# Moving part of a modulation product from TensorE to VectorE in a two-block transformer kernel

## The chip, the cores and the metric

One Trainium2 chip, one core. The metric is the device time in microseconds of one execution. The profile below is of one profiled execution of the kernel before.

## The reference, cut to what matters

Two transformer blocks run one after the other over 256 tokens of 1024 features, each of depth 2. The first block scales, shifts and gates its norms and branches with six vectors per layer that come from a single row `c` (1 x 1024) times a wide matrix:

```
for l in range(2):
    mod = c @ mod_w[l] + mod_b[l]                     # 1024 x 6144 per layer
    sh1, sc1, g1, sh2, sc2, g2 = split(mod, 6)
    h = rmsnorm(x, norm1_g[l]) * (1 + sc1) + sh1
    x = x + g1 * mixer(h, ...)
    h = rmsnorm(x, norm2_g[l]) * (1 + sc2) + sh2
    x = x + g2 * conv_ffn(h, w_up[l], ..., w_down[l])
```

All of it is float32, and the large products are made as three products of rounded halves (high x high, low x high, high x low).

## The kernel before, in words

`plan()` writes a list of steps; each engine walks the same list and executes its part of each step, so the order of the list is the order on every engine. Weights come from HBM in chunks of 1 MB, one DMA each, into a ring of 5 buffers (`RING`); SyncE issues the load of chunk c when chunk c-5 has been read. A chunk holds two weight blocks of 8 sub-matrices of 128 x 128. ScalarE rounds a block to `w_hi` (L1649) and VectorE subtracts to make `w_lo` (L2042); 6 blocks are held (`SPLIT`), and a block's place comes free only when the whole output tile that read it last is done. So in the down projection a burst of two or three splits follows the end of each tile.

A modulation chunk (the step `mod`) is another kind of 1 MB chunk: 1024 rows x 256 columns of `mod_w`, for one layer l, one of the six vectors g and a part 0 to 3 of it. TensorE multiplies `c` with it straight from the ring in 8 float32 matmuls of 32 columns, four side by side in the array (L1435); ScalarE copies the bank to `modacc` (L1698). After part 3, ScalarE writes the four rows to HBM with a 16 KB DMA (L1703, tile `mod_rows`). A later step, `modload`, is a DMA on ScalarE's queue that first waits until that write has landed and then reads the rows back transposed (L1710, tile `modv`); the step `modsum` on VectorE adds the four quarters and the bias.

These chunks are dealt out as filler by `some_mod`: one after each tile `dn` j of layer 0's down projection (j = 0 to 7, 22 sub-matrices each, 66 matmuls), two around each norm by `gap_mod`, one at places in the attention. `reduce_mod` puts `modload` or `modsum` into the list where the next `some_mod` or stage boundary is. Between the tiles stand the `stat` steps: ScalarE squares a finished tile of x (L1683), GpSimd adds the squares. After dn 7 comes `root` (TensorE sums over partitions, ScalarE L1688 and L1690, VectorE L2150 to L2156) and `norm` of layer 1 (VectorE L2182, ScalarE L1746), after which TensorE starts the products of layer 1. VectorE's x update of a finished dn tile is L2413.

At the very start of the kernel two modulation chunks are already multiplied by VectorE: 8 instructions over the row blocks of a chunk, one after another because each adds to the last (L2119, L2121, L2122).

## Time and profile before

| what | value |
|---|---|
| time, median of 3 runs (lowest to highest) | 1541.74 us (1539.85 to 1541.89) |
| the profiled execution: its own time | 1542.8 us |
| the profiled execution: span, mean granted TensorE clock | 1541.0 us, 0.993 |
| TensorE busy | 1496.3 us, 97% of the span |
| VectorE busy | 1143.7 us, 74% |
| ScalarE busy | 833.4 us, 54% |
| GpSimd busy | 31.4 us, 2% |
| layer 0's down projection, first to last x update of a tile | 403.13 to 465.43 us |

Busy shares say which engine carries the most work over the whole run; an idle stretch of TensorE is time lost only where it stands between two pieces of its own work. The windows and the timeline show this stage by stage.

### The profile page before, as it was taken

How to read it: one execution, taken by the hardware profiler on the slowest of the kernel's cores; microseconds unless marked ns; L12 is line 12 of the kernel's file. 1: busy time of each engine (PE TensorE's matmuls, PEld its weight loads, DVE VectorE, ACT ScalarE, POOL GpSimd, SP SyncE). 2: the span in 40 equal slices, each digit the busy share in tenths (PEclk: the TensorE clock that was granted, in tenths of full speed). 3: DMA queues.
4: the chain of work that ended last, by engine and by line, in shares of the span. 5: the costliest groups of instructions: out<-in, count | busy, mean ns of one | idle time of the engine just before them, and what ended most of it. 6: DMA issues, size and time to landing. Idle time of an engine off the chain costs nothing.

```text
span 1541.0 us, 31309 instructions
## 1 busy us (share of the span) xinstructions
PE 1496.3 (97%) x12608; PEld 1433.5 (93%) x12608; DVE 1143.7 (74%) x2202; ACT 833.4 (54%) x1509; POOL 31.4 (2%) x36
## 2 busy tenths in 40 slices
PE   6999999999999999999999999999999999999997
PEld 4898898999998999989999989999999999999997
DVE  5758566888646586769996678878966988888774
ACT  3655545655435646446555655645555754645453
POOL 0000001000000000010001000000000000000000
PEclk9999999999999999999999999999999999999998
DMA  9654555676776452454545543443446444444430
GB/s 393 251 216 184 202 223 192 219 275 247 275 272 252 168 214 87 157 196 165 179 179 194 219 164 113 169 185 138 154 152 246 150 154 163 167 163 141 169 129 28
DMA packets 47840, 290.51 MB, mean 189 GB/s; under 512 B 9992, under 2 KB 12296, under 8 KB 13136
## 3 DMA queue, kind: packets, MB, share of 16 engines
q1 hardware_dynamic: 38880, 280.83, 49.0%
q10 hardware_dynamic: 8816, 7.67, 1.5%
q8 instruction: 101, 1.65, 0.4%
q14 instruction: 43, 0.35, 0.1%
HBM read 286.09 MB, written 2.39 MB: 187 GB/s over the span
## 4 chain that ended last, share of the span: by engine, by line
PE 57%; DVE 1%; ACT 1%; DMA 0%; issue 0%; DVEq 0%; ACTq 0%
PE bank L1351 17%; PE bank L1357 16%; PE bank L1352 16%; PE bank L1601 2%; PE sums L1526 1%; PE sums L1416 1%; PE bank L1390 1%; PE bank L1395 1%; PE bank L1389 1%; PE bank L1508 1%; PE bank L1499 1%; DMA mem_x<-mem_t 0%; DVE w_lo L2042 0%; ACT w_hi L1649 0%; PE bank L1533 0%
## 5 line engine op out<-in xcount | busy, mean ns | idle before, releaser
L1351 PE MATMUL bank<-h_hi,w_hi 128*128 128x256 f32 x2256 | 632.8, 288 | 8.9 <-ACT h_hi L1746 3.7
L1352 PE MATMUL bank<-h_hi,w_lo 128*128 128x256 f32 x2256 | 622.3, 283 | 0.0
L2042 DVE TENSOR_TENSOR w_lo<-ring,w_hi 128x1024 fp32r<-128x1024 f32 x436 | 523.4, 1222 | 106.4 <-ACT w_hi L1649 103.8
L1357 PE MATMUL bank<-h_lo,w_hi 128*128 128x256 f32 x2256 | 575.9, 283 | 0.0
L1649 ACT ACTIVATE w_hi<-ring 128x1024 fp32r<-128x1024 f32 x436 | 449.2, 1054 | 131.4 <-PE bank L1357 130.9
L1351 PEld LDWEIGHTS bank<-h_hi,w_hi 128*128 128x128 f32 x2256 | 432.8, 192 | 22.9 <-issue 17.9
L1352 PEld LDWEIGHTS bank<-h_hi,w_lo 128*128 128x128 f32 x2256 | 433.0, 192 | 0.6 <-issue 0.5
L1357 PEld LDWEIGHTS bank<-h_lo,w_hi 128*128 128x128 f32 x2256 | 405.2, 192 | 0.0
L1351 PE MATMUL bank<-a_hi,w_hi 128*128 128x256 f32 x352 | 99.6, 283 | 1.0 <-DVE w_lo L2042 0.7
L1352 PE MATMUL bank<-a_hi,w_lo 128*128 128x256 f32 x352 | 98.3, 279 | 0.0
L1357 PE MATMUL bank<-a_lo,w_hi 128*128 128x256 f32 x352 | 98.2, 279 | 0.0
L1389 PE MATMUL bank<-w_hi,h_hi 128*128 128x256 f32 (+1 forms) x304 | 86.6, 289 | 3.9 <-ACT h_hi L1746 2.9
L1390 PE MATMUL bank<-w_lo,h_hi 128*128 128x256 f32 (+1 forms) x304 | 85.7, 286 | 0.0
L1883 ACT ACTIVATE conv_a<-bank,sm 128x256 f32<-128x256 f32 x44 | 24.8, 564 | 105.2 <-PE bank L1357 105.2
L1395 PE MATMUL bank<-w_hi,h_lo 128*128 128x256 f32 (+1 forms) x304 | 81.7, 287 | 0.0
L1351 PE MATMUL bank<-y_hi,w_hi 128*128 128x256 f32 x288 | 79.3, 280 | 0.0
L1352 PE MATMUL bank<-y_hi,w_lo 128*128 128x256 f32 x288 | 78.8, 278 | 0.0
L1357 PE MATMUL bank<-y_lo,w_hi 128*128 128x256 f32 x288 | 75.7, 281 | 0.0
L1944 ACT ACTIVATE sig<-bank 128x256 f32<-128x256 f32 x80 | 30.3, 379 | 78.1 <-PE bank L1357 77.5
L1351 PEld LDWEIGHTS bank<-a_hi,w_hi 128*128 128x128 f32 x352 | 66.1, 188 | 4.7 <-issue 3.3
L1389 PEld LDWEIGHTS bank<-w_hi,h_hi 128*128 128x128 f32 x304 | 59.6, 196 | 7.2 <-issue 5.9
L1352 PEld LDWEIGHTS bank<-a_hi,w_lo 128*128 128x128 f32 x352 | 66.2, 188 | 0.0
(336 smaller groups left out, 2345.7 us busy)
## 6 DMA issues: line engine op xcount, KB each, us to landing
ring<-weights SPq DMA_DIRECT2D x266, 1024.0 KB, 4.9
pos_bias<-scratch ACTq DMA_DIRECT2D x4, 512.0 KB, 5.6
x<-x_t ACTq DMA_DIRECT2D x1, 1024.0 KB, 6.9
scratch<-line ACTq DMA_DIRECT2D x1, 1024.0 KB, 5.6
mem_x<-mem_t ACTq DMA_DIRECT2D x1, 1024.0 KB, 6.7
mem_second<-mem_t ACTq DMA_DIRECT2D x1, 1024.0 KB, 6.2
out_t<-x SPq DMA_DIRECT2D x2, 512.0 KB, 2.6
co<-const SPq DMA_DIRECT2D x1, 462.0 KB, 7.2
```

The source lines that it names most:

```text
L1351: pe.matmul(to, WH[:, b % SPLIT, o, :], hi[:, k, :], start=(i == 0), stop=False)
L1352: pe.matmul(to, WL[:, b % SPLIT, o, :], hi[:, k, :], start=False, stop=False)
L1357: last = pe.matmul(to, WH[:, b % SPLIT, o, :], lo[:, k, :], start=False, stop=(i == n - 1))
L1389: pe.matmul(o, q, WH[:, s:s + m.n, k, :], start=(k == 0), stop=False)
L1390: pe.matmul(o, q, WL[:, s:s + m.n, k, :], start=False, stop=False)
L1395: last = pe.matmul(o, q, WH[:, s:s + m.n, k, :], start=False, stop=(k == KD - 1))
L1416: m = pe.matmul(sums[:, 0:S], ones, hb[:, k, :], start=(st.n is None and k == 0), stop=(k == KD - 1))
L1601: m = pe.matmul(to[:, (2 * g + s) * P:(2 * g + s + 1) * P], k[half, g, s * P:s * P + P], q[half, g, t * P:t * P + P], start=True, stop=True)
L1649: act.activation(WH[:, b % SPLIT], ring_half(b), ACT.Copy).then_inc(w_hi, 1)
L1883: act.activation(to[:, st.j % 3, :], bank[u.bank][:, 0:S], ACT.Identity, scale=ss(("conv_w", st.l, 2), c), bias=ss(("conv_b", st.l), c)).t ...
L1944: act.activation(sig2[:, st.j % 4, :], bank[st.ps.bank][:, 0:S], ACT.Tanh, scale=0.5).then_inc(taken[st.ps.bank], 1)
L2042: ve.tensor_tensor(WL[:, b % SPLIT], ring_half(b), WH[:, b % SPLIT].bitcast(F32), ALU.subtract).then_inc(w_lo_v, 1)
```

## The change

`mod` has a second form, `by_vector`, in which VectorE multiplies and adds the 8 row blocks of the chunk and leaves 128 partial sums per column in `modacc`. A new step `modrow`, put into the list at the next `some_mod`, adds these over the partitions with one float32 matmul against ones, and ScalarE copies the bank back to `modacc` with a factor 0.25, since `modsum` adds four rows. `gap_mod` does nothing while such a chunk is open, and `some_mod` returns early when its `mod_row` has completed a vector. It is asked for in layer 0's down projection for j < 6.

```
+BY_VECTOR = 6
...
-    def mod(l, g, part):
+    def mod(l, g, part, by_vector=False):
...
+        n = p.count("mod_rows") if part == 3 else p.counts.get("mod_rows", 0)
+        more = dict(v=p.count("mod_v"), eng="vector") if by_vector else dict(ps=p.full_bank(), after=state["parts"])
+        st = p.add("mod", chunk=len(p.chunks) - 1, l=l, g=g, part=part, n=n, **more)
+        if by_vector:
+            state["row"] = st
+            return
...
+    def mod_row():
+
+        st, state["row"] = state["row"], None
+        if st:
+            row = p.add("modrow", l=st.l, g=st.g, part=st.part, n=st.n, v=st.v, ps=p.full_bank(), after=state["parts"])
+            state["parts"].append(row.ps)
+            if st.part == 3:
+                state["summed"] = (st.l, st.g)
...
-    def some_mod(n=1):
+    def some_mod(n=1, by_vector=False):
         reduce_mod()
+        mod_row()
+        if state["summed"]:
+            return
         for _ in range(min(n, len(queue))):
             l, g, part = queue.pop(0)
-            mod(l, g, part)
+            mod(l, g, part, by_vector)
...
     def gap_mod():
-        if queue and not state["summed"]:
+        if queue and not state["summed"] and not state["row"]:
             mod(*queue.pop(0))
...
             ps = fm("dn", dn[j], j=j, l=l).ps
-            some_mod()
+            some_mod(by_vector=l == 0 and j < BY_VECTOR)
...
+            def modrow(st):
+                to = claim(st.ps)
+                pe.wait_ge(mod_v, st.v + 1)
+                pe.matmul(to[:, 0:256], ones, modacc[:, st.part, :], start=True, stop=True).then_inc(ready, 1)
...
+            def modrow(st):
+                wait_ready(act, st.ps)
+                act.activation(modacc[:, st.part, :], bank[st.ps.bank][:, 0:256], ACT.Copy, scale=0.25).then_inc(
+                    taken[st.ps.bank], 1)
+                if st.part == 3:
+                    for u in st.after:
+                        wait_taken(act, u)
+                    act.dma_start(mod_rows.ap()[st.n], modacc[0:97:32, :, :]).then_inc(mod_row_out, 16)
...
             def mod(st):
                 if st.eng != "vector":
                     return
+                if st.n is not None:
+                    ve.wait_ge(mod_row_out, 16 * st.n)
                 wait_loaded(ve, st.chunk)
```

ScalarE from the evacuation after dn 6 to the norm of layer 1, before (L1698 is the copy of a modulation bank, L1683 a square, L1688 the root's logarithm, L1710 the read-back):

```order
L1698 ACTIVATE modacc<-bank 128x256 [waits bank_ready]
L1703 DMA mod_rows<-modacc 4x1024 [waits bank_taken1,bank_taken3,bank_taken6,bank_taken4]
L1683 ACTIVATE h_val<-x 128x256 [waits bank_taken0]
L1649 ACTIVATE w_hi<-ring 128x1024 [waits bank_ready,chunk_loaded1]
L1649 ACTIVATE w_hi<-ring 128x1024 [waits bank_ready,chunk_loaded2] x2
L1710 DMA modv<-mod_rows 128x4x8 [waits mod_summed,mod_row_out]
L1698 ACTIVATE modacc<-bank 128x256 [waits mod_row_out,bank_ready]
L1683 ACTIVATE h_val<-x 128x256 [waits bank_taken2]
L1683 ACTIVATE h_val<-x 128x256 [waits bank_taken4]
L1688 ACTIVATE guess<-sums,co 128x256 [waits sums_ready]
```

The same stretch now (L1716 is the copy of a `modrow` bank, L1729 that of a modulation bank, L1734 the write of the rows, L1741 the read-back, L1705 a square, L1710 the logarithm):

```order
L1716 ACTIVATE modacc<-bank 128x256 [waits bank_ready]
L1729 ACTIVATE modacc<-bank 128x256 [waits bank_ready]
L1705 ACTIVATE h_val<-x 128x256 [waits bank_taken5]
L1671 ACTIVATE w_hi<-ring 128x1024 [waits bank_ready,chunk_loaded4]
L1671 ACTIVATE w_hi<-ring 128x1024 [waits bank_ready,chunk_loaded2] x2
L1729 ACTIVATE modacc<-bank 128x256 [waits bank_ready]
L1734 DMA mod_rows<-modacc 4x1024 [waits bank_taken2,bank_taken4,bank_taken1,bank_taken6]
L1705 ACTIVATE h_val<-x 128x256 [waits bank_taken0]
L1705 ACTIVATE h_val<-x 128x256 [waits bank_taken3]
L1741 DMA modv<-mod_rows 128x4x8 [waits mod_summed,mod_row_out]
L1710 ACTIVATE guess<-sums,co 128x256 [waits sums_ready]
```

The write of the rows of vector 4 has moved from after dn 6 to after dn 7, and its read-back from before the last two squares to directly before the logarithm.

VectorE at dn 5 and dn 6, before (L2413 is the x update of a tile; L2047 on `modv` is `modsum`, which stood between the x updates of dn 4 and dn 5):

```order
L2413 SCALAR_TENSOR_TENSOR x<-bank,modv,x 128x256 [waits bank_ready,mod_summed]
L2042 TENSOR_TENSOR w_lo<-ring,w_hi 128x1024 [waits w_hi_done] x3
L2413 SCALAR_TENSOR_TENSOR x<-bank,modv,x 128x256 [waits bank_ready]
L2042 TENSOR_TENSOR w_lo<-ring,w_hi 128x1024 [waits w_hi_done] x3
L2413 SCALAR_TENSOR_TENSOR x<-bank,modv,x 128x256 [waits bank_ready]
L2042 TENSOR_TENSOR w_lo<-ring,w_hi 128x1024 [waits w_hi_done] x4
L2047 TENSOR_TENSOR modv<-modv 128x16 [waits mod_cols_in]
```

Now (L2446 is the x update, L2073 the low halves, L2152 to L2155 the new product, L2078 on `modv` is `modsum`):

```order
L2446 SCALAR_TENSOR_TENSOR x<-bank,modv,x 128x256 [waits bank_ready]
L2073 TENSOR_TENSOR w_lo<-ring,w_hi 128x1024 [waits w_hi_done] x3
L2078 TENSOR_TENSOR modv<-modv 128x16 [waits mod_cols_in]
L2078 TENSOR_TENSOR modv<-modv 128x8 [waits vector_order]
L2078 TENSOR_TENSOR modv<-modv,sm 128x8 [waits vector_order]
L2152 TENSOR_SCALAR modacc<-ring,sm 128x256 [waits chunk_loaded2,mod_row_out,mod_summed]
L2154 SCALAR_TENSOR_TENSOR modacc<-ring,sm,modacc 128x256 [waits vector_order] x6
L2155 SCALAR_TENSOR_TENSOR modacc<-ring,sm,modacc 128x256 [waits vector_order]
L2446 SCALAR_TENSOR_TENSOR x<-bank,modv,x 128x256 [waits bank_ready]
L2073 TENSOR_TENSOR w_lo<-ring,w_hi 128x1024 [waits w_hi_done] x3
L2446 SCALAR_TENSOR_TENSOR x<-bank,modv,x 128x256 [waits bank_ready]
L2073 TENSOR_TENSOR w_lo<-ring,w_hi 128x1024 [waits w_hi_done] x4
```

The product stands behind the splits of its tile, and after dn 5 behind `modsum` of vector 2 as well. There are five such products, after dn 0, 1, 2, 4 and 5: after dn 3 the step `modrow` completes vector 2 and no chunk is taken. `modsum` of vector 4, which stood right before the root's VectorE part, now comes after the first rotation of layer 1's queries.

TensorE after dn 6, now (L1446 is the sum over the partitions, L1457 the modulation matmul, L1368 and L1374 those of the down projection):

```order
L1374 MATMUL bank<-a_lo,w_hi 128x256
L1446 MATMUL bank<-modacc,co 128x256 [waits mod_by_vector,bank_taken1]
L1457 MATMUL bank<-ring,c_wide 32x256 [waits chunk_loaded0,c_wide_ready,bank_taken2]
L1457 MATMUL bank<-ring,c_wide 32x256 x7
L1368 MATMUL bank<-a_hi,w_hi 128x256 [waits w_lo_by_vector,bank_taken3]
```

Before, one group of 8 modulation matmuls stood after each of dn 0 to 7; now there is an L1446 after dn 1, 2, 3, 5 and 6, and a group of 8 after dn 6 and dn 7. All modulation chunks that follow move down the list by one to three steps, and the last of them, which stood in the gap of layer 1's second norm, now stands after the second tile of the up projection.

## Rows read from the trace of the kernel before

**Rows 1.** The page: busy time, share of the span and instructions of each engine.
```profile
PE 1496.3 (97%) x12608; PEld 1433.5 (93%) x12608; DVE 1143.7 (74%) x2202; ACT 833.4 (54%) x1509; POOL 31.4 (2%) x36
```
**Rows 2.** VectorE's timeline, down projections of layers 0 and 1: start us, us, what.
```profile
456.53 0.48 DVE L2413 SCALAR_TENSOR_TENSOR x<-bank,modv,x 128x256 f32<-128x256 f32 x1 [4.95 <-PE bank L1357]
456.93 3.49 DVE L2042 TENSOR_TENSOR w_lo<-ring,w_hi 128x1024 fp32r<-128x1024 f32 x3
465.43 0.48 DVE L2413 SCALAR_TENSOR_TENSOR x<-bank,modv,x 128x256 f32<-128x256 f32 x1 [5.01 <-PE bank L1357]
...
858.66 0.48 DVE L2413 SCALAR_TENSOR_TENSOR x<-bank,modv,x 128x256 f32<-128x256 f32 x1 [4.95 <-PE bank L1357]
...
866.37 0.48 DVE L2413 SCALAR_TENSOR_TENSOR x<-bank,modv,x 128x256 f32<-128x256 f32 x1 [3.82 <-PE bank L1357]
```
**Rows 3.** TensorE's timeline at a float32 sum over the partitions (two matmuls, second block).
```profile
1027.69 0.70 PE L1582 MATMUL bank<-conf_out,co 128*128 128x256 f32 x2
1028.23 0.59 PE L1583 MATMUL bank<-conf_out,co 128*128 128x256 f32 x2
...
1028.78 0.28 PE L1352 MATMUL bank<-h_hi,w_lo 128*128 128x256 f32 x1
```
**Rows 4.** VectorE's timeline at the start: a modulation chunk multiplied by VectorE.
```profile
13.40 0.35 DVE L2119 TENSOR_SCALAR modacc<-ring,sm 128x256 f32<-128x256 f32 x1 [4.42 <-DMA ring<-weights]
13.79 3.09 DVE L2121 SCALAR_TENSOR_TENSOR modacc<-ring,sm,modacc 128x256 f32<-128x256 f32 x6
...
17.31 0.15 DVE L2047 TENSOR_TENSOR modv<-bank,sm 128x2 f32<-128x2 f32 x1
```
**Rows 5.** VectorE's timeline at both `modsum`, and GpSimd's at the first.
```profile
441.40 0.81 DVE L2047 TENSOR_TENSOR modv<-modv 128x16 f32<-128x16 f32 x2
...
470.37 0.37 DVE L2047 TENSOR_TENSOR modv<-modv 128x16 f32<-128x16 f32 x2
...
441.45 0.74 POOL L1246 TENSOR_TENSOR mean<-mean,h_val 128x256 f32<-128x256 f32 x1 [7.13 <-ACT h_val L1683]
```
**Rows 6.** Three 1 MB loads issued within 1 us: their time to landing.
```profile
L1309 SPq DMA_DIRECT2D ring<-weights x3: 328/423/424, 450.5 to 451.4; - x3
...
DMA to landing us min/median/max: 4.8/6.9/8.9
```
**Rows 7.** ScalarE's timeline from dn 6 to the norm of layer 1.
```profile
459.45 0.36 ACT L1698 ACTIVATE modacc<-bank 128x256 f32<-128x256 f32 x1
459.92 0.50 ACTq L1703 DMA_DIRECT2D mod_rows<-modacc  x1
460.46 0.42 ACT L1683 ACTIVATE h_val<-x 128x256 f32<-128x256 f32 x1 [0.65 <-ACT modacc L1698]
...
468.61 0.71 ACT L1683 ACTIVATE h_val<-x 128x256 f32<-128x256 f32 x2
470.23 0.47 ACT L1688 ACTIVATE guess<-sums,co 128x256 f32<-128x256 f32 x1 [0.91 <-PE sums L1416]
```
**Rows 8.** The line of the read-backs: all ten, and their time to landing.
```profile
L1710 ACTq DMA_DIRECT2D modv<-mod_rows x10: 361/362/381, 135.1 to 693.7; - x10
...
DMA to landing us min/median/max: 1.8/3.9/5.4
```
**Rows 9.** VectorE's timeline: the root's first instruction at that norm.
```profile
471.05 0.42 DVE L2150 TENSOR_SCALAR mean<-sums 128x256 f32<-128x256 f32 x1
```
**Rows 10.** TensorE's timeline: its restart after that norm, and a wait in layer 1's up projection.
```profile
474.05 0.36 PE L1389 MATMUL bank<-w_hi,h_hi 128*128 128x256 f32 x1 [2.00 <-ACT h_hi L1746]
...
699.53 0.38 PE L1351 MATMUL bank<-h_hi,w_hi 128*128 128x256 f32 x1 [1.35 <-DVE w_lo L2042]
```
**Rows 11.** Windows: busy us (instructions) of PE, PEld, DVE, ACT, POOL, then PEclk, DMA share, GB/s.
```profile
471.00:475.20 4.20, 2.20 (x29) 1.57 (x22) 3.88 (x11) 1.79 (x5) 0.00 (x0) 0.99 1.00 419
475.20:478.40 3.20, 3.20 (x17) 3.20 (x16) 3.20 (x10) 2.07 (x5) 0.00 (x0) 0.50 1.04 440
```

More of the change, by code:

```diff
@@ L188, in plain @@
         return p.matrix([tile_cols(name, lead, [(c0 + P * j, P)], rows) for j in range(n)])
-    state = dict(parts=[], summed=None, loaded=None, added={}, all_by_pe={})
-    def mod(l, g, part):
+    state = dict(parts=[], summed=None, loaded=None, added={}, all_by_pe={}, row=None)
+    def mod(l, g, part, by_vector=False):
         p.chunks.append(("mod", (l, g, part)))
-        st = p.add("mod", chunk=len(p.chunks) - 1, l=l, g=g, part=part, ps=p.full_bank(),
-                   n=p.count("mod_rows") if part == 3 else p.counts.get("mod_rows", 0), after=state["parts"])
+        n = p.count("mod_rows") if part == 3 else p.counts.get("mod_rows", 0)
[4 more added lines that the diff above has]
+            return
         state["parts"].append(st.ps)
@@ L1625, in from_h @@
                 linear([(claim(st.ps)[:, 0:S], st.subs)], XH, XL)
-            do = dict(bias=bias, root=root, norm=norm, mem_again=mem_again, mod=mod, modred=modred, tm=tm, tr=tr,
+            do = dict(bias=bias, modrow=modrow, root=root, norm=norm, mem_again=mem_again, mod=mod, modred=modred, tm=tm, tr=tr,
                       cum=cum, idx=idx, qkf=from_h, gate1=from_h, lg=lg, tp=tp, pv=pv, ot=ot, y1=y1, wo1=wo1, up=up,
@@ L2010, in hgn @@
                 act.activation(hb[:, 6:8, :], hb[:, 6:8, :], ACT.Exp, scale=-0.5).then_inc(hg_guess, 1)
-            do = dict(setup=setup, bias=bias, mod=mod, modload=modload, stat=stat, root=root, norm=norm, mem_again=mem_again, load_mem=load_mem, tm=tm, decay=decay, idx=idx, tr=tr, decay2=decay2,
+            do = dict(setup=setup, bias=bias, mod=mod, modrow=modrow, modload=modload, stat=stat, root=root, norm=norm, mem_again=mem_again, load_mem=load_mem, tm=tm, decay=decay, idx=idx, tr=tr, decay2=decay2,
                       qkf=qkf, gate1=gate1,
```

## The prediction

> **What bounds the kernel now.** I read the page first: TensorE is busy 97% of the span [rows 1], so time is gained where its work shrinks inside a stream, and lost where it waits. Then VectorE's timeline of layer 0's down projection: the x update of a tile follows the end of that tile on TensorE by 0.1 us, so the distance between two updates is the period of a tile. With a modulation chunk behind each tile it is 465.43 - 456.53 = 8.90 us; in layer 1, where none is left, 866.37 - 858.66 = 7.71 us [rows 2]. After its update VectorE makes the three low halves and is done 3.9 us after the update's start (456.93 + 3.49 - 456.53), then idles for some 5 us [rows 2]. Third, ScalarE's timeline into the norm of layer 1: there TensorE has only filler, and the chain square, sum, logarithm, root, h decides [rows 7, 10]. D is below the start of a tile's x update.
>
> **Not six but five chunks.** The order says that after dn 3 the step `modrow` completes vector 2 and `some_mod` returns. So five chunks go to VectorE (after dn 0, 1, 2, 4, 5).
>
> **TensorE in the down projection.** Before, 7 groups of modulation matmuls stand between dn 0 and the end of dn 7, each worth 8.90 - 7.71 = 1.2 us, 8.4 in all. After it there are one group (after dn 6) and five single float32 matmuls. The trace of before has no such matmul in this place; the nearest rows are the two of the same shape (ones, 128 x 128, 256 columns) between other work: from the start of the first to L1352, the second product of the stream behind them, 1028.78 - 1027.69 = 1.09 us, of which the first takes 0.54 [rows 3]. (One stream product, 7.71 / 66 = 0.12 us, lies inside that distance; I set it against the entry ahead of it.) A single one lies between 0.54 and 1.09. I take 0.64: the pair less the second one, which adds 1028.78 - 1028.23 - 0.12 = 0.43. New: 5 x 0.64 + 1.2 = 4.4. Gain **4.0 us**; a price of 0.54 makes it 4.5, one of 1.09 makes it 1.8.
>
> **VectorE in the down projection.** The chain of 8 takes 17.31 - 13.40 = 3.9 us, since each of them waits for the last [rows 4]. It stands behind the splits, so it ends at D + 3.9 + 3.9 = D + 7.8. TensorE wants it one tile later, at D - 0.1 + 0.64 + 7.7 = D + 8.2. So it fits with 0.4 us to spare after dn 0, 1, 4 (two splits at dn 0 and 4: more). Two exceptions.
> - After dn 5 `modsum` stands ahead of the chain; it took from 441.40 past 442.2, about 0.9 to 1.0 us, with GpSimd's add beside it [rows 5]. The chain ends at D + 8.8: TensorE waits **0.6 us**.
> - After dn 2 GpSimd's add falls into the chain: the square that feeds it begins 3.3 to 3.9 us after the update [rows 2, 7]. The pair of tiny adds took 0.81 us with GpSimd's 0.74 us add beside it and 0.37 without [rows 5]; so a stretch of 0.4 to 0.7 is to be had, the spare 0.4 is used up, and TensorE waits **0.3 us** (0 to 0.4). The Trainium skill's page "SBUF — State Buffer" (section "SBUF: two separate sides") says that a VectorE instruction with two SBUF inputs and a GpSimd instruction exclude one another for a whole instruction; by that rule the stretch is the whole add where it begins first, 0.7 us. The trace agrees in kind (0.81 against 0.37). After dn 4 the spare is larger and hides it.
>
> **The ring.** A slot that held a modulation chunk is now free when VectorE has read it, up to 7 us later than before. Worked through by the rule that chunk c waits for c-5: the weight chunks still land before their splits. One doesn't fit: the chunk for the group after dn 6 is issued second of two behind the second split of dn 5, at D5 + 0.4 + 2.35 + 0.4 = D5 + 3.1, and the second of loads issued together lands 6.9 us after its issue [rows 6], at D5 + 10.0. TensorE comes to it at D5 + 8.2 + 0.6 + 0.64 = D5 + 9.4. Another **0.6 us** (0 to 1.5). So dn 7 ends 4.0 - 1.5 = 2.5 us earlier than before.
>
> **The norm of layer 1: a wait is added.** Before, the rows of vector 4 were written after dn 6 and had all of dn 7 to land. Now the write follows dn 7, and its read-back, which waits for the landing, stands on ScalarE directly ahead of the root's logarithm. ScalarE takes its queue in order, so the logarithm, and behind it the root, h and TensorE's restart, wait for a DMA to HBM that none of them needs. Sizes: after dn 6 the copy began at D + 2.9, the write was issued at 459.92 = D + 3.4, and the next square came at D + 3.9 [rows 2, 7]. After dn 7 the pattern is the same, so issue at D + 3.4. The squares end at D + 4.7 and their sums would allow the logarithm at D + 5.6 (before: squares from 468.61, logarithm 470.23 = D + 4.8). The landing of this write is not in any view; the nearest rows are the read-backs, on the same queue and of the same 16 KB: 1.8 / 3.9 / 5.4 us from issue to landing [rows 8]. I take 4.8, the upper half, because in the same microsecond three 1 MB loads are issued (of the slots freed by the splits at D + 2.8 and by the two groups of TensorE), and the windows show DMA at a share of 1.00 here [rows 11]. Then the read-back issues at D + 8.2 and, 0.36 us long [rows 8], lets the logarithm go at D + 8.6: **3.8 us** later (0.8 at a landing of 1.8, where the squares decide; 4.4 at 5.4).
> The Trainium skill's page "DMA: Bandwidth & Descriptors" (section "Anatomy of one DMA — SWDGE (gpsimd) path") gives a fixed cost of about 2.0 us plus bytes over 436 GB/s for a DMA, fitted on another issuing path; by it the write would land after 2.0 us and the wait would shrink to about 1.0. The same page ("Latency and other measured facts") lets HBM's latency grow under load; the spread of rows 8 agrees with that.
>
> **Back on the credit side.** `modsum` of vector 4 no longer stands ahead of the root on VectorE: it held the first instruction until 471.05, 0.35 us after the logarithm's end at 470.70 [rows 7, 9]: **-0.25**. In its new place VectorE has slack; nothing.
>
> **Fillers further on.** In both norm gaps there are two groups before and after, in TensorE's idle time; three in the attention before and after. One group (1.2 us) now stands in the stream of layer 1's up projection. Before, TensorE waited 1.35 us there for a low half [rows 10], made by ScalarE and VectorE after a table load; the group runs inside that wait. ScalarE's copy and write (0.36 and 0.5 us) then delay a later split by what is in reserve. **+0.1** (0 to 1.2).
>
> **Sum.** -4.0 + 0.3 + 0.6 + 0.6 + 3.8 - 0.25 + 0.1 = **+1.15 us** on a profiled execution of 1542.8 us, itself 1.1 us above the median. On the median: 1541.74 + 1.15 = **1542.9 us**. A measurement of this kernel can tell about 0.2%, 3.1 us; so this is no change, with the gain of the down projection given back in one wait.
>
> **Rivals.**
> - *The write lands early* (1.8 to 2.0 us). The logarithm goes at D + 5.6, set by the squares: 3.0 less, 1539.9; without the three small waits as well, 1538.4. For it: most rows in quiet stretches; against: the load here. By the page's 2.0 us it would be this case. Chance 0.13.
> - *The write queues behind the loads.* If the loads of that moment go ahead of it as the third of three, 8.9 us [rows 6], the logarithm goes at D + 12.7, 4.1 more: 1547.0, slower by 0.34%. It decides from a landing of 6.8 us on. For it: DMA share 1.0; against: no 16 KB transfer took over 5.4. Chance 0.12.
> - *The clock.* After this norm TensorE ran 3.2 us and more at the granted 0.50 (1.2 GHz) before it was back at 2.4 GHz [rows 11], after a stretch with 2.20 of 4.20 us busy. TensorE now idles 3 to 4 us longer. The restart (474.05 + about 1.1) falls to where the low stretch began before, so I count nothing. A second low stretch while busy costs half of 3.4 us, 1.7: 1544.6. Chance 0.13.
>
> **How the numbers follow.** My forecast has 0.62, with its own range 1540.4 to 1545.0 (landing 3.8 to 5.4, matmul 0.54 to 1.09, the small waits). Faster by over 0.2% (under 1538.7) needs an early landing and no other wait: 0.07. Slower by over 0.2% (above 1544.8): the late write 0.12, half of the clock case, and the forecast's own tail, together 0.21. The range 1539.4 to 1546.2 leaves out the fastest corner and most of the late write.
>
> **What would show it.** Right: tile periods of 8.3 us after dn 1 to 3; five matmuls L1446; a small wait of them for the chain after dn 5; the x update of dn 7 about 2.5 us earlier; then the logarithm 8 to 9 us after that update instead of 4.8, with no work on ScalarE between the squares and it; one idle stretch of TensorE of 4 us or more; in the up projection a wait of 0.2 instead of 1.35. Wrong: a logarithm at D + 5.6, waits at every L1446 (chain too long), weight chunks that come late, or a low clock past 479 us.

## The result and the profile after

The change takes **1546.78 us** (median of 22 runs, 1542.82 to 1549.80) against 1543.25 us before (22 runs): ratio **1.0020, 95% interval 1.0014 to 1.0027**, some 3.1 us slower where +1.15 was forecast. (The three runs of before shown ahead of the prediction had a median of 1541.74; with 22 it is 1543.25. So 1.5 us of the miss in the absolute number belongs to its starting point, and 2 us or more to the change.) The profiled execution took 1547.66 us, its span 1545.9 at a mean clock of 0.990. Two single runs of the experiments below, one of 1818.82 us (before, busy gap) and one of 3690.81 us (read-back, modsum, copy behind), are slow ones and stand in no median or mean here.

Busy shares are as before [rows 1]:

```profile
PE 1494.5 (97%) x12538; PEld 1435.7 (93%) x12538; DVE 1164.0 (75%) x2242; ACT 832.7 (54%) x1509; POOL 31.6 (2%) x36
```

TensorE's busy time fell by 1.8 us, and the program got longer: what was saved in its stream came back as waits and, as shown below, as work at a lower clock. VectorE's timeline in layer 0's down projection (start us, us, what), to be read against [rows 2, 4]:

```profile
424.23 0.35 DVE L2152 TENSOR_SCALAR modacc<-ring,sm 128x256 f32<-128x256 f32 x1
424.62 3.45 DVE L2154 SCALAR_TENSOR_TENSOR modacc<-ring,sm,modacc 128x256 f32<-128x256 f32 x6
428.10 0.48 DVE L2155 SCALAR_TENSOR_TENSOR modacc<-ring,sm,modacc 128x256 f32<-128x256 f32 x1
428.65 0.48 DVE L2446 SCALAR_TENSOR_TENSOR x<-bank,modv,x 128x256 f32<-128x256 f32 x1
...
439.82 0.83 DVE L2152 TENSOR_SCALAR modacc<-ring,sm 128x256 f32<-128x256 f32 x1
...
448.65 0.92 DVE L2078 TENSOR_TENSOR modv<-modv 128x16 f32<-128x16 f32 x2
...
453.32 0.48 DVE L2155 SCALAR_TENSOR_TENSOR modacc<-ring,sm,modacc 128x256 f32<-128x256 f32 x1
453.72 0.48 DVE L2446 SCALAR_TENSOR_TENSOR x<-bank,modv,x 128x256 f32<-128x256 f32 x1
...
464.15 0.48 DVE L2446 SCALAR_TENSOR_TENSOR x<-bank,modv,x 128x256 f32<-128x256 f32 x1 [6.55 <-PE bank L1374]
```

The eight x updates stand 7.70, 8.13, 8.22, 8.50, 7.70, 8.87 and 10.43 us apart instead of some 8.90 each, 59.55 in all against 62.30. The period after dn 1 holds one matmul and no wait: 8.13 - 7.70 = 0.43 us. The updates at 428.65 and 453.72 start as the product ends, no longer as their tile ends. GpSimd's add falls into the product (0.83 instead of 0.35 us at 439.82):

```profile
439.60 0.90 POOL L1263 TENSOR_TENSOR mean<-mean,h_val 128x256 f32<-128x256 f32 x1 [5.78 <-ACT h_val L1705]
```

After dn 5, `modsum` stands ahead of the product, and TensorE pays there twice, first for the product, then for a load:

```profile
444.65 0.59 PE L1446 MATMUL bank<-modacc,co 128*128 128x256 f32 x2
...
453.95 0.67 PE L1446 MATMUL bank<-modacc,co 128*128 128x256 f32 x2 [0.94 <-DVE modacc L2155]
455.13 1.07 PE L1457 MATMUL bank<-ring,c_wide 128*32 128x256 f32 x16 [0.51 <-DMA ring<-weights]
```

ScalarE's timeline into the norm of layer 1 (before: [rows 7]):

```profile
467.54 0.52 ACTq L1734 DMA_DIRECT2D mod_rows<-modacc  x1
468.10 0.72 ACT L1705 ACTIVATE h_val<-x 128x256 f32<-128x256 f32 x2 [0.67 <-ACT modacc L1729]
472.86 0.39 ACTq L1741 DMA_DIRECT2D modv<-mod_rows  x1
473.30 0.47 ACT L1710 ACTIVATE guess<-sums,co 128x256 f32<-128x256 f32 x1 [4.48 <-DMA mod_rows<-modacc]
```

ScalarE idles 4.48 us for the landing of `mod_rows`. Its read-back goes 472.86 - 467.54 = 5.3 us after the write's issue, and the logarithm 9.15 us after the last x update where it stood at 4.80. TensorE's timeline shows what hangs on it (before: [rows 10]):

```profile
468.57 1.13 PE L1433 MATMUL sums<-h_val,co 128*128 128x256 f32 x4 [2.40 <-ACT h_val L1705]
469.63 1.07 PE L1457 MATMUL bank<-ring,c_wide 128*32 128x256 f32 x16
471.84 1.07 PE L1457 MATMUL bank<-ring,c_wide 128*32 128x256 f32 x16 [1.14 <-DMA ring<-weights]
476.88 0.41 PE L1406 MATMUL bank<-w_hi,h_hi 128*128 128x256 f32 x1 [3.96 <-ACT h_hi L1777]
...
704.19 0.39 PE L1368 MATMUL bank<-h_hi,w_hi 128*128 128x256 f32 x1 [0.17 <-DVE w_lo L2073]
```

Cut at its marks, the span divides so (us; the second profile is of the same kernel, the first experiment):

| stretch | before | change | change, second profile |
|---|---|---|---|
| start to the first x update of layer 0's down projection | 403.13 | 404.60 | 402.29 |
| from there to TensorE's restart after the norm | 70.92 | 72.28 | 72.03 |
| to the first x update of layer 1's attention output | 186.12 | 187.68 | 187.70 |
| to the first x update of layer 1's down projection | 157.18 | 157.47 | 157.46 |
| to the last one | 56.71 | 56.14 | 56.41 |
| to the end | 666.93 | 667.69 | 666.90 |

The first row is scatter: both profiles of one kernel differ by 2.3 us there, 1.9 of it by 35 us from the start, behind a wait for a load near 30 us (4.29 against 0.95 us). From the first x update to the end the change takes 3.4 and 2.6 us longer than before. The second row is what the prediction worked out: **+1.1 to 1.4**. The third it did not count: **+1.6 us** in a stretch in which TensorE executes the same 1538 matmul records. Windows over it, of before and then of the change (columns as in [rows 11]):

```profile
474.05:660.17 186.12, 183.00 (x1538) 176.99 (x1539) 122.94 (x305) 97.20 (x210) 0.00 (x0) 0.99 0.43 161
```

```profile
477.00:480.40 3.40, 3.40 (x17) 3.40 (x18) 3.40 (x10) 2.00 (x5) 0.00 (x0) 0.50 1.01 409
476.88:664.56 187.68, 184.49 (x1538) 178.49 (x1539) 123.69 (x309) 97.11 (x210) 0.00 (x0) 0.98 0.42 156
555.50:559.00 3.50, 3.50 (x19) 3.50 (x18) 3.18 (x14) 0.00 (x0) 0.00 (x0) 0.51 0.12 52
```

Before has one stretch of 3.4 us at the granted clock 0.50 (1.2 GHz) in it, at 475.1; the change has two, at 477.0 right with the restart and at 555.5. Over all runs the mean clock was 0.9908 for the change. The clocks of the 22 runs of before are not on record; its four groups of runs beside the experiments have 0.9925 to 0.9929 (one run at 0.945 left out). Time goes with clock: the 8 of the 22 runs of the change at 0.992 or more have a median of 1544.40 us, the other 14 one of 1547.49.

### The profile page after: what moved, and what is told of

It reads as the page before. It is cut to its first block, busy times and chain, and to the rows that moved or that the text cites. A ratio compares the mean times of both kernels' runs of the same rounds, so it can differ in the third digit from the quotient of the medians.

```text
span 1545.9 us, 31212 instructions
## 1 busy us (share of the span) xinstructions
PE 1494.5 (97%) x12538; PEld 1435.7 (93%) x12538; DVE 1164.0 (75%) x2242; ACT 832.7 (54%) x1509; POOL 31.6 (2%) x36
## 4 chain that ended last, share of the span: by engine, by line
PE 58%; DVE 1%; ACT 1%; issue 0%; DVEq 0%; ACTq 0%
PE bank L1368 17%; PE bank L1374 16%; PE bank L1369 16%; PE bank L1623 2%; PE sums L1548 1%; PE sums L1433 1%; PE bank L1407 1%; PE bank L1412 1%; PE bank L1406 1%; PE bank L1530 1%; PE bank L1521 1%; ACT w_hi L1671 0%; DVE w_lo L2073 0%; PE bank L1555 0%; PE bank L1636 0%
## 5 line engine op out<-in xcount | busy, mean ns | idle before, releaser
L1368 PE MATMUL bank<-h_hi,w_hi 128*128 128x256 f32 x2256 | 635.2, 289 | 7.7 <-ACT h_hi L1777 3.7
L2073 DVE TENSOR_TENSOR w_lo<-ring,w_hi 128x1024 fp32r<-128x1024 f32 x436 | 523.9, 1223 | 104.8 <-ACT w_hi L1671 101.9
L1374 PE MATMUL bank<-h_lo,w_hi 128*128 128x256 f32 x2256 | 578.0, 284 | 0.0
L1368 PEld LDWEIGHTS bank<-h_hi,w_hi 128*128 128x128 f32 x2256 | 434.6, 193 | 22.1 <-issue 18.3
L1374 PEld LDWEIGHTS bank<-h_lo,w_hi 128*128 128x128 f32 x2256 | 406.8, 193 | 0.0
L1368 PE MATMUL bank<-a_hi,w_hi 128*128 128x256 f32 x352 | 100.0, 284 | 0.3 <-DVE a_lo L2078 0.3
L1374 PE MATMUL bank<-a_lo,w_hi 128*128 128x256 f32 x352 | 98.4, 279 | 0.0
L1368 PE MATMUL bank<-y_hi,w_hi 128*128 128x256 f32 x288 | 79.4, 281 | 0.0
L1374 PE MATMUL bank<-y_lo,w_hi 128*128 128x256 f32 x288 | 75.8, 281 | 0.0
L1368 PEld LDWEIGHTS bank<-a_hi,w_hi 128*128 128x128 f32 x352 | 66.2, 188 | 1.4 <-issue 0.8
```

The lines of the kernel that those rows point to most:

```text
L1368: pe.matmul(to, WH[:, b % SPLIT, o, :], hi[:, k, :], start=(i == 0), stop=False)
L1374: last = pe.matmul(to, WH[:, b % SPLIT, o, :], lo[:, k, :], start=False, stop=(i == n - 1))
L2073: ve.tensor_tensor(WL[:, b % SPLIT], ring_half(b), WH[:, b % SPLIT].bitcast(F32), ALU.subtract).then_inc(w_lo_v, 1)
```

## The experiments

Each was timed in 10 to 12 runs beside the kernel before on the same chip (four groups of experiments, each on a chip of its own, so ratios compare across groups and medians do not). "Restart" is the restart of TensorE after layer 1's first norm, counted from the first x update of layer 0's down projection.

| kernel | median us (before beside it) | ratio, 95% interval | mean clock | restart |
|---|---|---|---|---|
| change again | 1547.03 (1543.41) | 1.0021, 1.0013 to 1.0030 | 0.9898 | 72.03 |
| read-back behind the norm | 1540.14 (1543.41) | 0.9982, 0.9969 to 0.9995 | 0.9925 | 69.69 |
| the same, again | 1542.62 (1543.41) | 0.9996, 0.9987 to 1.0004 | 0.9915 | 69.05 |
| before without turn 3 | 1547.37 (1543.41) | 1.0024, 1.0012 to 1.0035 | 0.9902 | 73.66 |
| part 3 by TensorE | 1543.87 (1543.41) | 0.9999, 0.9991 to 1.0007 | 0.9919 | 70.52 |
| change, busy gap | 1545.39 (1543.11) | 1.0017, 1.0008 to 1.0027 | 0.9933 | 72.02 |
| before, busy gap | 1543.15 (1543.11) | 1.0002, 0.9993 to 1.0010 | 0.9934 | 70.92 |
| read-back behind, busy gap | 1540.83 (1543.11) | 0.9993, 0.9984 to 1.0003 | 0.9932 | 68.90 |
| two chunks | 1544.72 (1543.11) | 1.0012, 1.0003 to 1.0021 | 0.9923 | 70.64 |
| two chunks, again | 1544.29 (1543.41) | 1.0012, 1.0004 to 1.0021 | 0.9925 | 70.39 |
| read-back and modsum behind | 1540.69 (1543.41) | 0.9983, 0.9975 to 0.9992 | 0.9928 | 69.04 |
| three chunks, read-back behind | 1543.95 (1543.41) | 0.9997, 0.9985 to 1.0009 | 0.9927 | 68.89 |
| read-back, modsum, copy behind | 1541.47 (1543.77) | 0.9987, 0.9978 to 0.9996 | 0.9921 | 69.45 |
| three chunks, read-back, copy behind | 1539.81 (1543.77) | 0.9980, 0.9970 to 0.9990 | 0.9927 | 68.38 |

Two profiles of the same kernel agree in every period of the down projection within 0.02 us, except where a load lands; between the fastest and the slowest run of one kernel lie 3 to 9 us. So the small terms are read from the profiles, and the medians decide only over 1 to 1.5 us.

**The change again, and the read-back moved.**

```
+    i = next(i for i, st in enumerate(p.steps) if st.kind == "modload" and (st.l, st.g) == (1, 4))
+    k = next(k for k in range(i, len(p.steps)) if p.steps[k].kind == "norm")
+    p.steps.insert(k, p.steps.pop(i))
```

> The changed kernel as it is, beside the others on one chip. Theory 1 (the wait for the written rows alone): +1.4 us against before at the restart of TensorE after the norm of layer 1, and about +1.2 at the end. Theory 2 (the clock pays the rest): the median is about 3 us slower, and the profile shows more or longer stretches at the granted 0.50 than that of before, each worth 1.7 us, with the spans of runs falling as the mean clock rises. Theory 3 (later stages pay): the profile shows a loss of 1 us or more in a stage after the restart while the clock is at 1.00.

> The changed kernel with the read-back of vector 4 moved behind the norm step; all arithmetic the same. Theory 1: the logarithm starts 5.6 us after the x update of dn 7 instead of 9.15, the copy of the next modulation bank then waits for the rows and delays h a little, TensorE restarts 9.7 us after that update instead of 12.7: 3.0 us faster than the changed kernel, 1.5 us faster than before. If the clock pays for the longer idle time (theory 2), it is 3 us plus up to 1.7 us faster than the changed kernel. If a rival were right that the squares or sums come late, the logarithm would stay at 8 us or more.

> The change with the read-back behind the norm, a second time, without filler. Theory: 3 us below before as the first time (restart 69.7 us behind the first x update of the down projection against 70.9, no low-clock stretch on the busy stream behind it, the 0.72 us wait at 826 gone); ratio 0.998. Rival (the first result owed 1 to 2 us to stretches of low clock that fell on idle time by chance): ratio 0.999, 1.5 us below.

The loss is reproduced (+3.6), and both theories have a share: the restart is 1.1 us later (theory 1), and none of these 12 runs reached a clock of 0.992, where 27 of the 35 of before beside them did (theory 2). With the read-back behind the norm the restart comes 2.3 us earlier than in the change, and the kernel is 6.9 us faster than the change beside it and 3.3 us faster than before; the second time the restart comes 3.0 us earlier than in the change, and the kernel stands 0.8 us below before, which its interval does not tell from nothing. So the place of the read-back was the origin of the loss: moving it alone takes the loss away. How much the cure is worth beyond that is scatter: in the first profile the low stretch fell on the idle time and the root's sums (469.1 to 472.5), and the stretch behind the restart took 184.71 us; in the second a low stretch ran on past the restart and another came at 550, and it took 187.63. In the first, the sums themselves doubled to 2.08 us:

```profile
469.55 2.08 PE L1436 MATMUL sums<-h_val,co 128*128 128x256 f32 x4 [2.40 <-ACT h_val L1708]
```

That is why its logarithm came 6.53 us after the last x update and not at 5.6, where the second has it. The second one's timeline of ScalarE has one more thing in it:

```profile
467.83 0.47 ACT L1713 ACTIVATE guess<-sums,co 128x256 f32<-128x256 f32 x1 [0.91 <-PE sums L1436]
...
470.92 0.39 ACT L1732 ACTIVATE modacc<-bank 128x256 f32<-128x256 f32 x1 [2.17 <-DMA mod_rows<-modacc]
471.20 0.89 ACT L1780 ACTIVATE h_hi<-h_val,modv 128x256 fp32r<-128x256 f32 x2
```

The copy of the next modulation bank waits for the same landing and stands ahead of h.

**Before, with the turn after dn 3 left out**, which moves the write of the rows behind dn 7 as the change does, with no product on VectorE.

```
-            some_mod()
+            if l or j != 3:
+                some_mod()
```

> The kernel before, nothing on VectorE, but no modulation chunk is taken after dn 3, so that vector 4 ends after dn 7 as in the changed kernel. Theory 1: dn 7 ends 1.2 us earlier, the logarithm starts 9.1 us after its x update (before 4.8), TensorE restarts 2.9 us later than before, and the whole is 2.9 us slower (0.19%). If the loss belongs to VectorE's product and not to the shift of the chunks, it is within 1 us of before.

```profile
469.81 0.50 ACTq L1704 DMA_DIRECT2D mod_rows<-modacc  x1
...
475.00 0.36 ACTq L1711 DMA_DIRECT2D modv<-mod_rows  x1
475.40 0.47 ACT L1689 ACTIVATE guess<-sums,co 128x256 f32<-128x256 f32 x1 [4.33 <-DMA mod_rows<-modacc]
```

The lost turn alone makes the wait (landing again after 475.00 - 469.81 = 5.2 us): dn 7 ends 1.2 us earlier, the restart is 2.7 us later (2.9 forecast), the time 4.0 us longer, the mean clock down to 0.9902. VectorE's product has no part in this wait.

**No lost turn: part 3 of a vector stays with TensorE.**

```
-            mod(l, g, part, by_vector)
+            mod(l, g, part, by_vector and part != 3)
```

> The changed kernel with part 3 of each vector left to TensorE, so that no turn is skipped: five chunks by VectorE again, vector 4 complete after dn 6 as before. Theory 1: the logarithm is back at 4.8 us after the x update of dn 7; five groups of 1.2 us become five matmuls of 0.43 us, 3.8 us less, minus waits for the chain of up to 1 us: restart 3 to 3.8 us earlier than before, 2.8 to 3.8 us faster than before (0.18 to 0.25%). If the product on VectorE itself costs more than it gives, it is no faster than before.

A miss: the restart is 0.4 us earlier than before, not 3 to 3.8, and the time is the same. The write has its old place and the logarithm stands at D + 4.8 again, but dn 7 ends only 0.6 us earlier than before. Seven groups became five matmuls and two groups, worth 8.4 - 2.15 - 2.4 = 3.8 us; waits ate 3.2 of it. TensorE waits 0.77 us for a product that GpSimd's add has stretched, the group after dn 6 waits 1.05 us for its load, and in the gap behind the root the filler's load is 2.04 us late, so that the restart at 474.89 stands directly behind filler:

```profile
438.51 0.67 PE L1446 MATMUL bank<-modacc,co 128*128 128x256 f32 x2 [0.77 <-DVE modacc L2155]
...
473.89 1.07 PE L1457 MATMUL bank<-ring,c_wide 128*32 128x256 f32 x16 [2.04 <-DMA ring<-weights]
```

**TensorE kept busy around the norm**, in the change, in before (3 and 4 matmuls) and in the form with the read-back moved (4 and 2). The filler's results are overwritten.

```
+FILL_ROOT = {2: 4}
+FILL_NORM = {2: 7}
...
+                for _ in range(FILL_NORM.get(new, 0)):
+                    pe.matmul(to[0][:, 0:S], ones, co[:, 0:S], start=True, stop=True)
...
+                for _ in range(FILL_ROOT.get(st.i, 0)):
+                    pe.matmul(sums[:, S:2 * S], ones, co[:, 0:S], start=True, stop=True)
```

> The change with TensorE kept busy around the norm: 4 float32 matmuls (0.43 us each at 2.4 GHz) ahead of the root's sums, in the 2.4 us wait, and 7 (3.0 us) behind the last modulation group, in the 3.1 to 4.0 us wait; their results are overwritten. The chain to the restart is untouched. Theory (part of the loss is the clock: each stretch granted 0.50 that falls on busy work costs half of 3.4 us): the low stretch behind the restart (477.0 to 480.4 in the change) goes, perhaps that at 555 too; 1.7 to 3.4 us less than the change, ratio to before 1.000 +- 0.0005; restart as in the change within 0.3 us. Rival (the idle time alone is the loss, the low stretches come whatever TensorE does): ratio to before stays at 1.002, and as many low stretches.

> The kernel before with the same filler: 3 matmuls (1.3 us) in the 1.6 us wait ahead of the last squares' sums, 4 (1.7 us) in the 2.0 us wait ahead of the restart. Theory: its one low stretch behind this norm goes, 1.7 us less, ratio 0.999; then the change with filler stands 1 to 1.3 us above this one, which is the loss without the clock. Rival: 0 +- 0.5 us.

> The change with the read-back behind the norm, and filler of 4 matmuls ahead of the root's sums and 2 ahead of the restart. Without filler the low stretch 469.1 to 472.5 doubled the four sums (2.08 instead of 1.13 us) and held the logarithm to D + 6.5. Theory: sums 1.1 us, logarithm at D + 5.6, restart 0.9 us earlier, 69.0 us behind the first x update of the down projection (before 70.9, change 72.1 to 72.3), no low stretch between 465 and 480 us; ratio to before 0.997 to 0.998. Rival (low stretches come anyway, the filler delays): ratio 0.998 to 0.999 and restart not earlier.

TensorE's timeline and the window behind it, of the change with filler:

```profile
471.30 3.29 PE L1402 MATMUL bank<-co 128*128 128x256 f32 x14
474.91 0.36 PE L1410 MATMUL bank<-w_hi,h_hi 128*128 128x256 f32 x1 [0.31 <-ACT h_hi L1783]
```

```profile
474.91:659.62 184.71, 181.51 (x1538) 175.51 (x1539) 123.62 (x308) 97.17 (x210) 0.00 (x0) 1.00 0.43 160
```

The restart did not move (72.02), both low stretches are gone, and the same work takes 184.71 us where it took 187.68: 3.0 us, 1.5 for each. So what a low stretch costs on busy work is shown in the profiles. The times followed only in part. The change with filler stands at 1.0017 of before (1.0008 to 1.0027), inside the interval of the change without it (1.0013 to 1.0030); the theory's 1.000 is missed and the time is nearer the rival's 1.002, though the clock rose from 0.9898 to 0.9933. The profiled execution is not a typical one: with 1542.79 us at a clock of 0.995 it was the third fastest of twelve, whose median is 1545.39. Before gained nothing (1543.15, the theory's 1.7 missed; its profile has a low stretch at 549.9 in place of the one at 475). Compared with each other, the two with filler have one clock (0.9933, 0.9934) and stand 2.2 us apart, where the theory had 1 to 1.3; without filler it is 3.6.

Runs of one clock say much the same. At 0.992 or more the medians are 1544.40 for the change (8 of 22 runs) against 1542.70 for before (27 of the 35 runs beside the second timing), and 1545.14 for the change with filler (10 of 12 runs) against 1542.85 for before beside it (29 of 35). So 1.7 to 2.3 us of the 3.6 remain at one clock, and the rest goes with the clock. This split is an estimate from few runs: the intervals with and without filler overlap. What remains is more than the 1.1 to 1.4 us that the restart shows, and where the difference arises is not settled.

The count of low stretches goes the same way, profile by profile, in the stretch from the restart to the first x update of the attention output. It took 187.68, 187.70 and 187.00 us in the three profiles with the wait for the write and no filler (the change twice, before without turn 3), and 186.12 to 186.26 us in the five in which the chain to the restart waits as before (before with and without filler, part 3 by TensorE, two chunks twice).

In the third form with filler, the sums took 1.13 us and the restart came 0.8 earlier than in the first run of that form (0.15 than in the second, whose sums were not slowed either), with no low stretch from 40 to 892 us, all as the theory had it; the ratio, 0.9993, was not the 0.997 to 0.998 forecast, and no gain in the time can be told.

**Only the first chunks by VectorE.** `BY_VECTOR = 3` on the form with part 3 by TensorE (two chunks, after dn 0 and 1), and on the form with the read-back moved (three).

> A smaller form of the change: VectorE multiplies only the chunks after dn 0 and dn 1 (parts 1 and 2 of vector 2), everything else is in the order of before, so the write of the rows and the read-back have their old places. Theory (the product pays where no ring slot is late and no turn is lost): two groups of 1.2 become two matmuls of 0.43, 1.5 us less at dn 7 and at the restart, ratio 0.999. Rival (late ring slots eat it, as the 1.05 and 2.04 us waits for loads did in the form with part 3 by TensorE): 0 to 0.5 us less, ratio 1.000, and a wait of TensorE for a load of 0.5 us or more after dn 2 or dn 3.

> VectorE multiplies two chunks only (after dn 0 and dn 1), a second time. The first profile showed its restart 0.3 us earlier than before, against a time 1.6 us longer. Theory (clock and start scatter made that 1.6): ratio 0.999 to 1.0005. Rival (a cost that the first profile did not show): ratio 1.001 again and a wait, or a low stretch on busy work, that before does not have.

> The change with VectorE's chunks cut from j < 6 to j < 3 (three products, after dn 0 to 2, then the lost turn after dn 3, then groups after dn 4 to 7), and the read-back behind the norm. Theory (the two products after dn 4 and dn 5 bring 1.5 us and cost 1.4 in two waits): three matmuls of 0.43 and three groups of 1.2 in place of seven groups less a wait of 0.3: periods 7.7, 8.13, 8.2, 8.2, then 8.9, dn 7 ends 3.3 us earlier than before instead of 2.7, restart at 68.7 to 69.3 behind the first x update, ratio 0.997 to 0.998. Rival (a late ring slot, as the 0.80 us wait of the form with two chunks): 0.8 of it is lost after dn 4, restart at 69.5 to 70.1, ratio 0.998 to 0.999.

Two chunks: the rival was right about the wait. The group after dn 2 waits for its load:

```profile
430.29 1.07 PE L1457 MATMUL bank<-ring,c_wide 128*32 128x256 f32 x16 [0.80 <-DMA ring<-weights]
```

That load was not held up by VectorE's slow reading. The product that had its slot was done at 419.78; the load was issued at 423.32, directly behind one at 422.94 that had waited for a low half, and as the second of the two it landed 6.8 us later (VectorE's timeline, and SyncE's two loads with the least and the greatest time to landing):

```profile
419.30 0.48 DVE L2155 SCALAR_TENSOR_TENSOR modacc<-ring,sm,modacc 128x256 f32<-128x256 f32 x1
...
L1326 SPq DMA_DIRECT2D ring<-weights x2: 328/376/425, 422.9 to 423.3; - x2
...
DMA to landing us min/median/max: 4.7/5.8/6.8
```

What put it there is the order of the chunks. `schedule()` in the kernel puts the weight chunks up to `st.upto` into the list ahead of a step, but only those up to `st.upto - 2` ahead of a `mod`; the new step `modrow` stands ahead of the next `mod` and does not count as one, so a weight chunk moves in front of the modulation chunk (first in front of part 2 of vector 2, in this kernel). With `modrow` counted like `mod` in that line the list of this kernel has the order of before again around these tiles; no run timed it. The 0.51 us wait of the change is of the same kind: its load went at 448.06, directly behind one at 447.68, and the product that had its slot was done at 444.3.

Dn 7 ends 0.6 us earlier, not 1.5. That both timings came out 0.12% above before although the restart is 0.3 to 0.5 us earlier is not explained. The clock does not do it: the runs at 0.992 or more have medians of 1544.26 and 1544.15 us against 1542.85 and 1543.01 for before. Both profiles had the late start (first x update at 404.3 and 404.7), whose share in the other runs can't be seen. Three chunks: no wait for a load, dn 7 after 59.25 us, 3.05 earlier than before, against 2.75 with five chunks. The last two products of the change brought nothing: 2 x (1.2 - 0.43) = 1.5 us, and 1.4 to 1.8 in waits. The restart, 68.89, is in the range forecast; the ratio, 0.9997, is not (0.997 to 0.998), with the widest scatter of all (1538.5 to 1547.7) and two low stretches behind the restart in its profile (187.62 us), as well as a third at 682.

**`modsum` behind the product after dn 5**, added to the form with the read-back moved.

```
+    i = next(i for i, st in enumerate(p.steps) if st.kind == "modsum" and (st.l, st.g) == (1, 2))
+    k = next(k for k in range(i, len(p.steps)) if p.steps[k].kind == "mod")
+    p.steps.insert(k, p.steps.pop(i))
```

> As the run before, and the sum of vector 2 on VectorE moved from ahead of the product after dn 5 to behind it. Theory (the two waits after dn 5 stand in a row behind one another: TensorE waits for the chain, 0.94 us, and then for the chunk of the next group, 0.5 us, whose landing does not depend on the first wait): the wait of the sum over the partitions shrinks to about 0.1, that for the load grows to 1.3, dn 7 ends as before it (period after dn 5 8.1 instead of 8.87, after dn 6 11.2 instead of 10.45), no gain: 0 +- 0.3 us. Rival (the waits add): dn 7 ends 0.8 us earlier, restart 0.8 us earlier.

```profile
452.40 0.67 PE L1452 MATMUL bank<-modacc,co 128*128 128x256 f32 x2 [0.27 <-DVE modacc L2161]
454.18 1.07 PE L1463 MATMUL bank<-ring,c_wide 128*32 128x256 f32 x16 [1.11 <-DMA ring<-weights]
```

The first wait fell from 0.94 to 0.27 and the second rose from 0.5 to 1.11; dn 7 ends 59.47 us after the first update instead of 59.5. The two waits hide one another. Its better time than the run beside it (1540.69 against 1542.62) is no merit of the move: from the first x update to the restart they take 69.04 and 69.05 us.

**The copy moved as well**: the modulation group between root and norm goes behind the norm on the list.

```
+    i = next(i for i in range(k - 1, 0, -1) if p.steps[i].kind == "mod")
+    p.steps.insert(k, p.steps.pop(i))
```

> The form with the read-back and the sum of vector 2 moved, and now also the modulation group between root and norm moved behind the norm on the list, so that ScalarE's copy of its bank, which waits for the same write of the rows (2.17 us in the profile of the form with the read-back moved) and stood ahead of h, comes behind h. TensorE's order is the same. Theory (the write's landing still held h there): restart 0.4 us earlier, 68.6 behind the first x update instead of 69.05, no wait of ScalarE for the write ahead of h; ratio 0.998. Rival (VectorE's part decides h): restart at 69.0 and the ratio as it was.

> The form with three chunks by VectorE and the read-back moved, and the same group moved behind the norm. Here the write is issued as late and lands as late, but that form's restart was 68.89 already. Theory: restart at 68.5 to 68.9, and with low-clock stretches on the stream behind it as by chance 0 to 2, ratio 0.997 to 0.9995, median below before. Rival (the longer wait ahead of the restart, 2.2 us there against 0 to 1.3, brings the two low stretches each time): ratio 0.9995 to 1.0005 again, with two low stretches behind the norm.

ScalarE's timeline in the form with three chunks:

```profile
467.17 0.47 ACT L1715 ACTIVATE guess<-sums,co 128x256 f32<-128x256 f32 x1 [0.91 <-PE sums L1438]
...
470.09 0.91 ACT L1782 ACTIVATE h_hi<-h_val,modv 128x256 fp32r<-128x256 f32 x2 [2.00 <-DVE h_val L2220]
```

From the logarithm to the restart it is now 3.57 us (3.58 in the other form) instead of 4.06: 0.5 us, the second victim of the landing. The first form's restart still stood at 69.45, not the 68.6 forecast, since a low stretch fell on the root's sums again (logarithm at D + 6.5). The form with three chunks has the earliest restart of all, 68.38. Its one low stretch near the norm (467.5 to 470.9) fell on filler, the next came at 890.7; that is in part luck, since the same form without this last move had three in those 400 us. Its time is the best: 1539.81, ratio 0.9980 (0.9970 to 0.9990), as the theory had it. It beats both kernels: before by 0.2%, and the change, which stands at 1.0020 of the same yardstick, by 0.4%.

## Why the prediction was wrong

The mechanism of the wait was right, and the sum to the restart nearly so: +1.0 worked out (-2.5 - 0.25 + 3.8), +1.1 to 1.4 measured. What was put at nothing, and failed, is the clock. By its steps:

- *Five chunks and not six; one group left; write behind dn 7, read-back ahead of the logarithm.* Right, as the order had it.
- *A single float32 matmul at 0.64 us.* It costs **0.43**. The pair less its second was taken, and the second's own price, 0.43, was the right one. Worth 1.05 us more.
- *Small waits, 0.3 + 0.6 + 0.6 = 1.5.* Measured 2.2 (59.55 less seven bare tiles of 7.71, less 1.2, less five times 0.43), with each of the three in its place: 0.37 after dn 3 (8.50 - 8.13), 0.94 and 0.51 after dn 6, the rest not placed. The 0.51 came as worked out, from the place of the load behind another, and not from VectorE's later reading. The product after dn 5 ended at D + 8.95 instead of D + 8.8 and TensorE took it up 0.15 us later still, a handover that the sum left out. So dn 7 ends 2.75 earlier instead of 2.5. That this fits so well is luck: two errors that nearly cancel.
- *GpSimd's add stretches the chain by up to the whole add.* The six products took 3.45 instead of 3.09 us, and the first of them 0.83 instead of 0.35: 0.36 and 0.48 us each, by adds shown as 0.90. The rule of the Trainium skill's page "SBUF — State Buffer" (section "SBUF: two separate sides"), that the two exclude one another, is borne out in kind, the size is not settled: when the product's first instruction came up at 439.82, 0.68 us of the add's span were left, and it lost 0.48.
- *The write lands after 4.8 us.* It took **5.3** and 5.1, near the upper end of [rows 8]: logarithm at D + 9.15 and D + 8.9, not 8.6. By the fixed cost of about 2.0 us that the Trainium skill's page "DMA: Bandwidth & Descriptors" gives (section "Anatomy of one DMA — SWDGE (gpsimd) path", for another issuing path), the landing would have held the logarithm by some 0.2 us beyond the squares and sums (an estimate: D + 5.8 against D + 5.6). The traces do not agree for this write: no instruction that waited for it went on sooner than 5.0 us after its issue.
- *The 1.35 us wait of the up projection takes up the displaced group.* Right: 0.17 us of it are left, and the whole stretch is 0.28 us longer (0.1 forecast). Not seen: a wait of 0.72 us in layer 1's down projection of before is gone from it as well, 0.3 to 0.6 us gained.
- *The clock, "so I count nothing".* **This is the step that failed.** It was a rival at 0.13 with a price of 1.7 us. Measured: one more low stretch on busy work in both profiles of the change, +1.6 us there, and mean clocks of 0.9908 and 0.9898 against 0.9927. In the times the clock's part comes to roughly 1.3 to 1.9 of 3.6 us, so it alone does not make up the whole miss either. I looked only at the place where the low stretch of before stood, and found it just as busy; the additional one came 80 us further on, at 555, behind a wait of 1.1 us that both kernels have.
- *The base.* A median of three runs was taken as the level of before. It was 1.5 us low.

The range (1539.4 to 1546.2) missed the time by 0.6 us; around the median of 22 runs the same terms would have given 1544.4 and 1540.9 to 1547.7.

Not settled: what decides that a low stretch begins, why the form with two chunks is 0.12% slower, and the part of the loss that remains at one clock beyond the later restart. Filling the waits around one norm left no low stretch in the next 400 us in two profiles (the change, and the form with the read-back moved) and only moved one in a third (before).

## What to carry to other kernels

Follow not the instruction that is moved but every instruction that waits for what it writes: here a 16 KB write that nobody needed soon, moved from 5.5 us before the last x update to 3.4 us behind it, held the norm through a DMA issue on ScalarE's queue, and behind that through a copy. Put such a read-back, and every copy that waits for it, behind the chain. Hand an idle engine only so much work as it finishes before the next thing in its queue is due: with three products the down projection was 3.05 us shorter, 1.2 of it by the turn left out, and the two further products were given back in waits for the product and for a load; since those waits hide one another, curing one shows nothing. When a step is added to a list from which the order of the loads is worked out, compare that order before and after. And where a change lengthens a wait of TensorE, put a price on one more low stretch on busy work, 1.4 to 1.6 us here, and do not look for it only next to the wait.

## What the runs showed of the hardware

- A single float32 matmul of 128 x 128 by 256 columns in a stream costs 0.43 us at 2.4 GHz; the same work behind the norm costs 184.71, 186.12 or 187.68 us with none, one or two stretches of 3.4 us at the granted clock 0.50 in it.
- A 16 KB write to HBM on ScalarE's queue, issued while SyncE issued three or four 1 MB loads within 2.6 us, let the instruction that waited for it go 5.0 to 5.8 us after its issue, in the nine profiles in which one did.
- A low stretch can come where TensorE had hardly idled: in the 13.5 us ahead of that at 555.5 it had one wait of 1.13 us. And a low stretch costs not only on the stream: where it fell on the four sums of the root (2.08 instead of 1.13 us) it delayed the logarithm by 0.9 us.
- Two profiles of one and the same kernel differ by 1.9 us by 35 us from the start, behind one wait for a load (4.29 against 0.95 us).
